# Two-layer hybrid trunk on one Trainium2 core: the modulation sums, the bias rows and the layer boundary reordered

## The reference

```
cond = silu(c)
shift, scale, gate = split(cond @ w_ada[layer] + b_ada[layer], 3)       # w_ada: 2048 x 6144 a layer
h = rms_norm(x, norm_g[layer]) * (1 + scale) + shift
... = split_columns(h @ w_in[layer])                                    # three branches: gated delta rule (a), conv (b), sparse attention (c)
merged = g_a * (y_a @ w_proj_a) + g_b * (y_b @ w_proj_b) + g_c * (y_c @ w_proj_c)
x = x + gate * (merged @ w_out[layer])
```

## Time and profile before

| | us |
|---|---|
| median of 3 runs | 2473.62 |
| range of the runs | 2473.61 to 2476.98 |
| profiled execution: time, span | 2470.99, 2469.2 |
| TensorE / VectorE / ScalarE / GpSimd busy | 2293.0 / 1250.3 / 949.4 / 1674.1 |
| mean granted TensorE clock | 0.959 |
| moved by DMA | 479.8 MB, mean 194 GB/s |

### The profile page before, as it was taken

The page is one execution under the profiler, slowest core; times in us unless marked ns, Lnnn a source line. Parts: engine busy times, 40 slices in busy tenths (PEclk is TensorE's granted clock), DMA queues, the critical chain, the costliest instruction groups (busy, mean ns, idle before and its releaser), DMA issues.

```text
span 2469.2 us, 37923 instructions
## 1 busy us (share of the span) xinstructions
PE 2293.0 (93%) x15224; PEld 2098.9 (85%) x15224; DVE 1250.3 (51%) x1742; ACT 949.4 (38%) x1014; POOL 1674.1 (68%) x676
## 2 busy tenths in 40 slices
PE   3789899989999979998896999998999999899999
PEld 3679899978889968786896999998788998688899
DVE  6749874745443474543434694764545437421110
ACT  2234344472332534343333444436423234344442
POOL 1358768755554778986775886876555558798876
PEclk7789999999999999999998999999999999999999
DMA  8877535443333569797774574554334335975664
GB/s 329 319 252 224 162 121 178 146 132 121 124 119 103 179 244 323 279 319 263 289 249 148 186 218 143 167 168 130 124 123 128 111 114 194 323 272 187 200 209 154
DMA packets 228326, 479.83 MB, mean 194 GB/s; under 512 B 21569, under 2 KB 25793, under 8 KB 219617
## 3 DMA queue, kind: packets, MB, share of 16 engines
q1 hardware_dynamic: 226880, 475.72, 57.2%
q10 hardware_dynamic: 1312, 2.23, 0.2%
HBM read 471.48 MB, written 6.29 MB: 193 GB/s over the span
## 4 chain that ended last, share of the span: by engine, by line
POOL 47%; issue 40%; PE 12%; POOLq 1%; DMA 0%; ACT 0%; DVE 0%; DVEq 0%; ACTq 0%
POOL wl L503 47%; PE ps L864 4%; PE ps L865 4%; PE ps L866 4%; POOLq L502 0%; PE ps L958 0%; DMA raw<-w_pb 0%; PE ps L1269 0%; POOLq L498 0%; ACT wh L524 0%; ACT gate L512 0%; DVE xs L1889 0%; DVE ps L1624 0%; POOLq L503 0%; DVEq L1307 0%
## 5 line engine op out<-in xcount | busy, mean ns | idle before, releaser
L503 POOL TENSOR_TENSOR wl<-raw,wh 128x1024 fp32r<-128x1024 f32 x672 | 1673.9, 2504 | 782.1 <-ACT wh L524 780.7
L524 ACT CAST wh<-raw 128x1024 fp32r<-128x1024 f32 x672 | 701.0, 1048 | 1275.2 <-PE ps L866 994.9
L864 PE MATMUL ps<-ah,wh 128*128 128x256 f32 x3008 | 873.3, 290 | 49.9 <-DVE al L1404 36.2
L865 PE MATMUL ps<-al,wh 128*128 128x256 f32 x3008 | 859.9, 286 | 0.0
L866 PE MATMUL ps<-ah,wl 128*128 128x256 f32 x3008 | 859.5, 286 | 0.0
L864 PEld LDWEIGHTS ps<-ah,wh 128*128 128x128 f32 x3008 | 587.0, 195 | 57.5 <-issue 22.5
L865 PEld LDWEIGHTS ps<-al,wh 128*128 128x128 f32 x3008 | 586.8, 195 | 4.7 <-issue 4.4
L866 PEld LDWEIGHTS ps<-ah,wl 128*128 128x128 f32 x3008 | 586.3, 195 | 0.0
L864 PE MATMUL ps<-wh,ah 128*128 128x512 f32 (+1 forms) x832 | 327.0, 393 | 28.1 <-POOL wl L503 28.1
L866 PE MATMUL ps<-wh,al 128*128 128x512 f32 (+1 forms) x832 | 320.0, 385 | 0.0
L865 PE MATMUL ps<-wl,ah 128*128 128x512 f32 (+1 forms) x832 | 319.9, 385 | 0.0
(11 more groups left out here) (254 smaller groups left out, 2057.7 us busy)
## 6 DMA issues: line engine op xcount, KB each, us to landing
raw<-w_in SPq DMA_DIRECT2D x512, 512.0 KB, 3.4
modw<-w_ada SPq DMA_DIRECT2D x64, 1024.0 KB, 5.7
adaw<-w_ada SPq DMA_DIRECT2D x32, 1024.0 KB, 7.5
raw<-w_out SPq DMA_DIRECT2D x64, 512.0 KB, 4.7
raw<-w_pc SPq DMA_DIRECT2D x32, 512.0 KB, 3.6
raw<-w_pb SPq DMA_DIRECT2D x32, 512.0 KB, 8.1
raw<-w_pa SPq DMA_DIRECT2D x32, 512.0 KB, 4.9
gbias<-b_gate SPq DMA_DIRECT2D x24, 256.0 KB, 4.2
```

Source lines behind the costliest of these rows:

```text
L503: nc.gpsimd.tensor_tensor(wl[:, s], raw[:, s], wh[:, s].bitcast(F32), ALU.subtract).then_inc(sem("w_split"), 1)
L524: A.copy(wh[:, s], raw[:, s]).then_inc(sem("w_rounded"), 1)
L864: M.matmul(o, lh, rh, start=start, stop=False, skip_group_check=True)
L865: M.matmul(o, lh, rr, start=False, stop=False, skip_group_check=True)
```

## The change

- Prologue: the bias products of all 8 heads run before the first quarter, into PSUM banks 0 to 3, with four `rbb` tiles and six stages. An ada tile now holds two row tiles of both parts (two DMAs of 512 KB, one slot), and one VectorE instruction covers shift and scale of a row tile, 1024 columns into two PSUM banks. `ada_sum` turns both parts at once. SP loads x and the parameters after the first four ada slots.
- Modulation units: the memsets go; unit 0 is a `tensor_scalar` that starts the sum; GATING's units 0 to 14 add up in PSUM.
- z stage: both reciprocals and the norm of `qg` come first, gating units 0 and 1 after `ub`, unit 2 after `yl`, unit 3 after y_a.
- Turn 3 of branch a: the wait for SHIFT's sum and its taking move behind SCALE units 0 and 1.
- Layer boundary: SCALE's partition sum moves behind the last w_out group; the last squares are taken and summed in halves of two row tiles (`x_half`); the reciprocal is written to PSUM (`rstp`, bank 5); ScalarE adds the shift and writes the high part (four instructions a quarter); VectorE forms the low part in one instruction a row tile (`shifted_low`).

```diff
             def ada_quarter(q):
-                for part in (SHIFT, SCALE):
-                    for j in range(4):
-                        n = 8 * q + 4 * part + j
-                        if n >= 4:
-                            sp.wait_ge(sem("ada_used"), n - 3)
-                        sp.dma_start(adaw[j][:], wa[0, :, 4 * j:4 * j + 4, part * D + q * GW:part * D + (q + 1) * GW]
-                                     ).then_inc(ada_landed[j], 16)
+                for j in range(8):
+                    n = 8 * q + j
+                    if n >= 4:
+                        sp.wait_ge(sem("ada_used"), n - 3)
+                    for part in (SHIFT, SCALE):
+                        col = part * D + q * GW
+                        sp.dma_start(adaw[j % 4][:, :, part], wa[0, :, 2 * j:2 * j + 2, col:col + GW]
+                                     ).then_inc(ada_landed[j % 4], 16)
+                    if n == 3:
+                        sp.dma_start(xs[:], xt.rearrange("p (k t) -> p k t", t=T)).then_inc(sem("x_landed"), 16)
+                        sp.dma_start(par[:], params).then_inc(sem("par_landed"), 16)
...
+            for h in range(4):
+                bias_row(h)
+            for h in range(HEADS):
+                act.wait_ge(sem("bias_mm"), h + 1)
+                if h + 4 < HEADS:
+                    bias_row(h + 4)
+                if h >= STAGES:
+                    act.wait_ge(sem(f"skew{h % STAGES}"), 16 * (h // STAGES))
+                A.copy(stage[:, h % STAGES, :], ps[:, h % 4, :]).then_inc(sem("bias_row"), 1)
+                act.wait_ge(sem("bias_row"), h + 1)
+                act.dma_start(skew[h], stage[:, h % STAGES, :]).then_inc(sem(f"skew{h % STAGES}"), 16)
...
                 def h_high(q):
+                    for kt in range(4 * q, 4 * q + 4):
+                        last = A.activation(ah[:, kt], merged[:, kt], ACT.Identity, bias=mods[:, kt:kt + 1])
+                    last.then_inc(sem("hh_ready"), 1)
...
-                    act.wait_ge(sem("x_done"), 4 * L1)
-                    A.activation(merged[:, 12:16], xs[:, 12:16], ACT.Square).then_inc(sem("sq_ready"), 1)
+                    for half in range(2):
+                        act.wait_ge(sem("x_half"), half + 1)
+                        at = 12 + 2 * half
+                        A.activation(merged[:, at:at + 2], xs[:, at:at + 2], ACT.Square
+                                     ).then_inc(sem("sq_ready"), 1)
...
-                             12: [lambda: sum_squares(L1, 2)], 14: [scale_sum]}
+                             12: [lambda: sum_squares(L1, 2)]}
                 group(1, H, before=steps)
                 if layer < DEPTH - 1:
-                    sum_squares(L1, 3)
+                    scale_sum()
+                    for half in range(2):
+                        sum_squares(L1, 3, half)
...
-                V.reciprocal(rst[:], rst[:])
+                V.reciprocal(rstp, rst[:])
...
+                def shifted_low(q):
+                    dve.wait_ge(sem("hh_ready"), 4 * layer + q + 1)
+                    for kt in range(4 * q, 4 * q + 4):
+                        m = V.scalar_tensor_tensor(al[:, kt], merged[:, kt], mods[:, kt:kt + 1],
+                                                   ah[:, kt].bitcast(F32), ALU.add, ALU.subtract)
+                    m.then_inc(sem("hT_ready"), 1)
...
                 o_recip(0)
-                V.memset(acc[:, 0], 0.0)
+                o_recip(1)
+                V.drain()
+                V.scalar_tensor_tensor(qg, qg, p_(layer, "gdn_g"), ors[:], ALU.mult, ALU.mult)
                 z_silu(4, 0, zs[0])
...
-                for n in (0, 1):
-                    mod_unit(n, passes[0] + n, n % 2, 0)
-
-                o_recip(1)
-                V.drain()
-                V.scalar_tensor_tensor(qg, qg, p_(layer, "gdn_g"), ors[:], ALU.mult, ALU.mult)
-                done("o_normed")
+                gating_units(0, 1)
                 dve.wait_ge(sem("yh_ready"), 3 * layer + 2)
                 V.tensor_tensor(yl[:], ub[:], yh[:].bitcast(F32), ALU.subtract).then_inc(sem("y_split"), 1)
+                gating_units(2)
                 z_silu(5, 1, zs[0])
                 hc += 4 * G_IN
                 V.scalar_tensor_tensor(qg, qg, 0.5, zs[0][:], ALU.mult, ALU.mult).then_inc(sem("ya_ready"), 1)
-                for n in (2, 3):
-                    mod_unit(n, passes[0] + n, n % 2, 0)
+                gating_units(3)
...
                     units(0)
+                    if last_a and layer < DEPTH - 1:
+                        dve.wait_ge(sem("mod_summed"), 3 * layer + 2)
+                        mods_from(layer + 1, SHIFT).then_inc(sem("shift_taken"), 1)
                     gate_add(i, hc, n0)
...
-                if not last_layer:
-                    dve.wait_ge(sem("mod_summed"), 3 * layer + 2)
-                    mods_from(layer + 1, SHIFT).then_inc(sem("shift_taken"), 1)
                 units = turn(3, "a", 12 * layer + 8, True)
```

More of the change, by code:

```diff
@@ L242, in trunk @@
         hotsb = sb("hotsb", 114, [2 * T])
-        rbb = sb("rbb", 116, [P])
-        stage = sb("stage", 118, [2, 2 * T])
+        rbb = sb("rbb", 116, [4, P])
+        stage = sb("stage", 118, [STAGES, 2 * T])
         ps = nc.alloc_psum_tensor("ps", [P, 8, 512], F32)
         pb = [ps[:, 4 + n, :] for n in range(4)]
+        rstp = ps[:, 5, T:2 * T]
         skew = nc.dram_tensor("skew", (HEADS, P, 2 * T), F32, kind="Internal").ap()
@@ L542, in _, with bias_row @@
             act.wait_ge(sem("con_landed"), 16)
[L543 to L557, removed]
+            def bias_row(h):
+                A.activation(rbb[0:BUCKETS, h % 4], ones[0:BUCKETS, :], ACT.Copy, scale=rbt[0:BUCKETS, h:h + 1]
+                             ).then_inc(sem("rbb_ready"), 1)
+            for h in range(4):
[9 more added lines that the diff above has]
+                act.dma_start(skew[h], stage[:, h % STAGES, :]).then_inc(sem(f"skew{h % STAGES}"), 16)
             act.sem_inc(sem("prep_wT"), 1)
@@ L977, in _ @@
                         pe.wait_ge(gemm_free[n], 1)
+                    pe.wait_ge(sem("bias_row"), HEADS)
                     for q in range(4):
-                        for part in (SHIFT, SCALE):
-                            ada_sum(q, part)
+                        ada_sum(q)
                         pe.wait_ge(sem("hT_ready"), q + 1)
@@ L1351, in ada_part, with mod_unit @@
                 dve.sem_inc(sem("ada_summed"), 1)
-            def mod_unit(kt, u, s, which, last=KT - 1):
+            def mod_unit(kt, u, s, which, last=KT - 1, first=UNIT_A):
                 V.drain()
@@ L1358, in mod_unit @@
                 wide = ps[:, 4:8, :]
[L1359 to L1362 removed]
+                o = wide if first <= kt < last else side
+                w = modw[s][:].rearrange("p (b n) -> p b n", b=4)
+                if kt == 0:
+                    unit = V.tensor_scalar(o, w, cond[:, 0:1], None, ALU.mult)
+                else:
+                    unit = V.scalar_tensor_tensor(o, w, cond[:, kt:kt + 1], wide if first < kt <= last else side,
+                                                  ALU.mult, ALU.add)
+                unit.then_inc(sem("mod_used"), 1)
             def mods_from(layer, part):
@@ L1832, in turn @@
                         k0 = 0 if i == 3 else i * 4
-                        if i == 3:
-                            V.memset(acc[:, 1 - part], 0.0)
                     def units(first):
@@ L1889, in _ @@
                         last = V.scalar_tensor_tensor(xs[:, n], o, gout[:, n:n + 1], xs[:, n], ALU.mult, ALU.add)
-                    last.then_inc(gemm_free[j % 2], 1)
+                        if j == 3 and not last_layer and ct % 2:
+                            last.then_inc(sem("x_half"), 1)
+                    if j == 3 and not last_layer:
+                        done(f"gemm_free{j % 2}")
+                    else:
+                        last.then_inc(gemm_free[j % 2], 1)
                     done("x_done")
```

107 lines of the change are left out of this document (50 added, 57 removed).

## The result

The changed kernel takes 2429.05 us (median of four runs, 2421.01 to 2431.41); the ratio to the kernel before is 0.9815, 95% interval 0.98 to 0.9829. It is faster, as forecast, but 18 us above the 2410.6 forecast and 1 us inside the upper end of the range, 2430. The profiled execution is the fastest of the four (2421.01 us, span 2419.2). The same kernel run again beside the first experiments gave 2433.59 (2430.11 to 2436.21), its profile a span of 2434.4; that median would have been outside the range, so the hit owes something to luck.

What follows compares the result with a forecast made beforehand. TensorE is busy 2293 of 2469 us, so only some 180 us of idle or slow-clock stretches can be won. Gains 9.5 + 32 + 12.5 + 9 = 63 from 2470.99, plus 2.6 for the median, give 2410.6 us; range 2396 to 2430.

Steps and rivals of the forecast that it cites:

- Prologue: 9.5 forecast: Prologue: wider steps and earlier start make quarter 3's low part end at 150.8, before 160.26; gain 9.5 us (2 to 14).
- Width, start and bias rows: Prologue: 1024-column steps of 1.36 us, first slot at 9.0, bias rows done at 47, quarter 1 at 59.6.
- What is late next is DMA: Prologue, quarters 1 to 3: each takes 30.4 us; 11.5 MB at 385 GB/s need 29.9, so faster VectorE gains no more.
- Rival 2: Prologue: bias rows up front eat the gain, quarters at 32 us for want of DMA; gain 0, total 2420, chance 0.13.
- a ceiling: Prologue: with 341 GB/s as the limit for ada loads, a quarter would be 34 us and the gain nothing.
- z stage: 16 a layer forecast: z stage, both layers: new order leaves 2.4 us lost in place of 18.4; gain 16 a layer (11 to 18).
- the time of `z_silu`: z stage: TensorE ends z_a near 876.1, `z_silu` is done at 879.4, y_a at 882.5, unit 3 at 885.
- rival 1: z stage: SP stays blocked, unit 3 runs at 893, not 885; 8 of each 16 us lost, total 2427, chance 0.15.
- under 12: z stage, sign to look for: SP's wait for units falls from 24.7 us to below 12.
- Turn 3 of a: 12.5 forecast: Branch a, layer 0: units no longer wait for SHIFT's sum, first transpose 11.8 us earlier; gain 12.5 us (10 to 15).
- Boundary: 9 forecast: Layer boundary: low part at 1313.2 against 1322.19; gain 9 us (4 to 14), 5.3 from halves and the moved sum.
- the case that the lock only moves to the low parts: Layer boundary: the VectorE-GpSimd lock moves whole from products to low parts; gain from halves and sum alone, 5.3 us.

Runs made afterwards that it cites:

- the control: The changed kernel run once more with no edit: 2433.59 us, ratio 0.9836 to the kernel before.
- the undone move: Changed kernel with the shift's 16 small products and their addition to mods again ahead of turn 3 of a: 2438.19 us, ratio 0.9868.
- all three orders at once: Changed kernel with x loaded ahead of the tiles, w_in chunks 4 and 5 deferred, loads of units 2 to 7 issued later: 2408.22 us, ratio 0.9744.
- whole scaling as before: Changed kernel with, at the layer boundary, reciprocal in SBUF, VectorE adding the shift, ScalarE casting a quarter at once: 2432.82 us, ratio 0.9829.

## Why the prediction was right, and where it was wrong

*Direction and terms.* Three places gained and the prologue about held. The forecast 63 us became 44.6 by the medians (2473.62 - 2429.05), and 39.2 by those of the control and the kernel before beside it (2472.82 - 2433.59), which would be 4 us outside the range. That the first measurement fell inside was luck as well as method.

*Prologue: 9.5 forecast, 2.7 and -1.0 measured.* Width, start and bias rows came near the forecast (1.36 a step, quarter 1 at 58.6). TensorE's small products took 3.71 of a quarter for 3.9. **The step that failed** is "What is late next is DMA" with its quarter of 30.4: I followed SP past the splits for quarter 0, and for the later quarters costed VectorE's chain and the bytes alone. SP's own order stood between. With chunks 4 and 5 deferred a quarter takes 29.9, close to the forecast's 30.4, and the low part of quarter 3 comes at 147.1, better than the 149.6 at which it was forecast to start (150.8 less 1.23). Rival 2 (the bias rows eat the prologue) has the right total, and its mechanism is a part of it: 3 us from the granted clock in the control, and 3 or more by x behind four slots. DMA as the bound of the 34 us is refuted. A table of the Trainium skill (DMA: Bandwidth & Descriptors, Measured) has 341 GB/s for a DMA of 1 MB, measured for DMAs issued from GpSimd; the prediction tried it as a ceiling, an estimate of 34 us a quarter. The changed kernel's quarters did take 34.1, 34.3 and 33.9, and yet not for that reason: 512 KB loads moved 386 GB/s over 30 us once SP let them go. An estimate can give the measured number and be wrong in its cause.

*z stage: 16 a layer forecast, 9 measured* (13.8 in layer 1 of the profile after, 9 in the others). Cause and direction were right: order 3.8 and 3.2, PSUM 1.2. Some 4 us a layer are explained by neither run alone; no run has both the old order and the old place, so whether the two together account for them is not shown. The term that was mis-sized is the time of `z_silu`. The forecast put it 3.3 us behind the end of z_a, at once; ScalarE's tanh for it stands behind the casts of gate chunks 2 and 3, and these wait for their loads behind units 2 and 3. So `z_silu` ends at 881.5 for 878.3 (the forecast's 879.4, less the 1.15 by which the stage starts earlier), unit 3 ends at 887.7 for 883.9, and chunk 6 is cast at 894.2 for some 890. Behind TensorE's wait for it the clock was 0.50 from 898 to 902 and 0.85 to 906, which the forecast had at nothing: an estimated 2.6 us at full clock. That is rival 1, at 0.15 too low, in part: SP waits 17.7 for units where I wanted under 12. Issuing the loads of units 2 to 7 two chunks later gives the stage 6.7 more, nearly all that the forecast had promised (9 + 6.7 = 15.7), but half of it is gone again behind b's turns.

*Turn 3 of a: 12.5 forecast, 8 to 14 measured*, 11 by the medians. Right, and the undone move gives 8 of them back. The 11.8 us of the transpose's wait became 12.27 - 1.32 = 10.95.

*Boundary: 9 forecast, 7.7 to 11.4 measured* (the `w_out` turns with the stretch behind them: 563.0 before, 555.3 in the control, 551.6 after). Right in sum, not in its parts. From the last additions TensorE starts 23.3 us later before, 17.2 after, but 20.1 in the control. The forecast gave TensorE's squares 2.8 us and let the scale's sum run beside the additions; in nine of twelve profiles the clock fell to 1.2 GHz during the sum, which runs ahead of the squares, so that both took longer (4.72 and 3.76 in the control), and the root came later than before. Products of 0.42 us with the reciprocal in PSUM, low parts of 1.48 beside the splits: a quarter's low part takes 5.9 where I took 6.9 (1306.3 to 1313.2). The Trainium skill (SBUF — State Buffer, Who interferes with whom) has VectorE and GpSimd lock each other out, and by it I had set the case that the lock only moves to the low parts. The measurement lies between: of 7.6 us taken from the products 3.3 reach TensorE. The scale's sum behind the last product frees 4.9 us in the `w_out` turns.

*What was missing altogether* is the spread. One code gave 2421 to 2436 us; the kernel before, in 27 runs, 2469 to 2478. Serial steps of TensorE that the change put on the path (the bias rows, the scale's sum) take their time by the granted clock; that explains 6.6 of the 15 us.

## What to carry to other kernels

When an engine is made faster, walk the queue that feeds it in its own order, one full period further than the stall that is removed: a load behind a wait costs nothing only while something else is later. Put loads that are needed late behind those that are needed soon, even where both fit; here three reorderings of loads gave 21 us on top of a change that gave 45. See whether a stage's gain is still there a stage later: half of one was not. And judge a part by the length of its own stretch in several profiles, since the totals moved by more than most parts.

## What the hardware showed unexpectedly

- Tiles of 512 KB with rows of 2 KB kept 386 GB/s over 30 us (all three orders at once, 84 to 114 us); the 34 us a quarter were not the size of a load.
- Small products of VectorE with two SBUF inputs beside GpSimd's splits took 2.3 us each (9.22 for four, whole scaling as before) in place of 0.42, about the time of one split; the next four, behind the splits, took 0.42 again (the 10.98 for eight are a mix of both). The splits' 9.6 us are met once, by whichever instructions come there: with the products out of the way, 4.3 of their 7.6 us went to the low parts.
- The fall of TensorE's clock came 2 us earlier in one execution than in another of the same code (mean 0.74 against 0.96 in the same five microseconds), which went with 3 us in the prologue; another such fall went with 3 at the boundary.
